# A fused three-layer block on Trainium2: the GQA value projection of the sequence tokens placed behind the key blocks, attention without a barrier, reciprocals computed on turned rows

## The chip, the cores and the metric

One core of one Trainium2 chip (trn2). The kernel is written in raw Bass: each engine has its own instruction stream, and semaphores alone order the streams. The metric is the device time in microseconds of one execution, as a median of several runs. PE is TensorE, DVE is VectorE, ACT is ScalarE, POOL is GpSimd; SP (SyncE) issues nearly all DMAs.

## The reference

One sequence of 256 tokens with 1024 features passes through a hybrid layer (Mamba-2 scan, sparse attention, a mixture of 32 experts) and then through two layers that work on the sequence (x) and on 256 context tokens: GQA with a convolutional FFN, then MLA with the same kind of FFN. All is float32. What the change touches:

```python
def rms_norm(x, g):
    return x * lax.rsqrt(jnp.mean(x * x, axis=-1, keepdims=True) + EPS) * g

def gqa_mixer(hx, hc, w_in, q_g, k_g, w_out, ctx_out):      # 16 query heads, 4 key heads, 64 wide
    def project(h):
        q, k, v = jnp.split(h @ w_in, splits, axis=-1)
        return rms_norm(q, q_g), rms_norm(k, k_g), v        # per head
    qx, kx, vx = project(hx)
    qc, kc, vc = project(hc)
    qx, kx = apply_rope(qx, cos, sin), apply_rope(kx, cos, sin)
    k_all, v_all = concat([kc, kx]), concat([vc, vx])
    out_x = softmax(qx @ k_all.T * scale) @ v_all @ w_out
    out_c = softmax(qc @ kc.T * scale) @ vc @ w_out
```

The scan's output is normed in four groups of 512 features; MLA norms its two low-rank projections.

## The kernel before

**Layout.** Activations lie feature-major: features on the 128 partitions, tokens along the columns. `hn` is the normed input, KD = 8 blocks of 128 features by 512 columns (T2), columns 0 to 255 (T) the sequence and 256 to 511 the context. Weights stream from HBM through six ring slots. SP waits for a slot to be freed (by PE or DVE) and issues the next DMA. `bank[0..7]` are the eight PSUM banks.

**A norm.** ACT squares (L1396), PE multiplies the squares with a matrix of ones (`sums`, L673), so that every partition holds the same sum for a token, ACT takes the square root into `rstd` (L1399), DVE takes its reciprocal (`norm`, L1891) and scales (L1896), ACT adds the shift (L1416) and PE uses `hn` block by block. Of these norms four are over 256 columns (first layer, before the experts, before the second FFN, the final one) and two over 512 (before the first FFN, before MLA). The scan does the same per group (`normed`, L2092, four times 256), MLA for its two projections (L2493 with 512, L2506 with 256), and between the experts and GQA two norms are done at once (L2433 and L2439, 256 each).

**GQA.** SP issues the value weights and the four `gqa` weight blocks between 921.2 and 923.4 us. PE computes the values for token tiles t = 2, 3 (context) and 0, 1 (sequence), eight matmuls each over the features, into banks 7 and 6; ACT copies both to `gva` (L1674) and signals `v_ready`. The context half of `hn` is ready early, the sequence half comes from the double norm. Then come twelve blocks c = 0 to 11: for each of KVG = 4 groups two blocks of query heads and one of keys. `block_step` is a software pipeline that stands on PE, ACT and DVE alike. At step c PE does the projection of block c into bank c % 3 (L647), for block c-1 the sum of squares within heads, **sums(c-1)** (L1191, bank 3), and for block c-2 the rope's rotation, **rot(c-2)** (L1197, bank 4). ACT squares block c (L1681) and takes the square root, **std(c-1)** (L1686, L1688). DVE takes the reciprocal, **recip(c-1)** (L2463), scales (L2466, then `q_normed`), and ropes block c-2 (L2472, L2474, L2476, then `q_roped`); L2474 needs rot(c-2). rot(c-2) waits for `q_normed` of the block after it and, since bank 4 is used again, for the rope of the block before. Steps 12 and 13 have no projection and only drain the pipeline. Then `end_phase()` makes PE, ACT and DVE wait for one another.

**Attention.** 32 pairs of heads and query tiles, again a pipeline: PE computes scores (L1213), DVE their maximum (L1976), ACT the exponentials (L1457), DVE the reciprocal of their sum and the scaling (L1984, L1992), PE transposes (L752), ACT copies (L1443), PE multiplies with the values (L1220). Scores(p) from the third pair on wait for the exponentials of pair p-2. The first pair's scores open the pipeline.

What sets the order is the program text of each engine; nothing is scheduled by a planner. The change touches the setup of the arena places (L397), PE's values, `block_step`, the barrier and `gqa_pair` (L1164 to L1222), ACT's copy (L1674) and barrier, and on DVE `norm`, `normed`, the double norm, `block_step`, the barrier and MLA's two reciprocals.

## Time and profile before

| what | us |
|---|---|
| median of 3 runs (2117.36 to 2120.48) | 2120.43 |
| the profiled execution | 2118.72 |
| its span, first to last instruction | 2116.9 |
| PE busy | 1971.0 (93%) |
| PE weight loads busy (beside PE) | 1382.5 (65%) |
| DVE busy | 1046.8 (49%) |
| ACT busy | 561.2 (27%) |
| chain that ended last: PE, DVE, DMA, waiting for nothing shown, ACT | 87%, 5%, 3%, 2%, 1% |
| mean granted clock of TensorE, share of full | 0.971 |

The profile records one execution. Busy time counts what an engine executes; the chain of work follows the last instruction back through whatever released it. The list of waits tells for each engine what it stood idle for and which instruction ended that. A name with q (DVEq) is the engine's own queue: a drain or a semaphore step of that engine ended the wait. Matmuls on float32 are recorded twice each, so 8 matmuls are 16 records. The granted clock is the share of TensorE's full 2.4 GHz; its low level, 1.2 GHz, is 0.5.

### The profile page before, as it was taken

The page shows a single profiled execution, that of the slowest core. Times are in us where ns is not written, and L with a number is a line of the kernel's source. Part 1 is how long each engine was busy: PE and PEld are TensorE (multiplying, and loading weights), DVE is VectorE, ACT ScalarE, POOL GpSimd, SP SyncE. Part 2 cuts the span into 40 slices and gives each one's busy share as a digit, 9 for nine tenths or more (in the row PEclk, how much of TensorE's full clock was granted, in tenths as well). Part 3 has the DMA queues.
Part 4 walks back from the last instruction along what each step waited for, and adds up shares of the span by engine and source line. Part 5 has one row for each costly group of instructions (what it writes and reads, how often), then busy time and mean ns, then how long its engine had stood idle before and what let it go on. Part 6 is the DMA issues. An engine that isn't in the chain of part 4 may idle for free.

```text
span 2116.9 us, 27563 instructions
## 1 busy us (share of the span) xinstructions
PE 1971.0 (93%) x9995; PEld 1382.5 (65%) x9995; DVE 1046.8 (49%) x2212; ACT 561.2 (27%) x1177; POOL 59.5 (3%) x68
## 2 busy tenths in 40 slices
PE   5999898789989999999799899999999898999997
PEld 4888687657755555564355388888444465778886
DVE  3466662367432222245676867777688334333311
ACT  3333300153131111131174133333000224443410
POOL 0000000000000000000000000101000010000000
PEclk9999999889999999999899999999999999999999
DMA  9345383232559999830102312223575020134451
GB/s 385 136 193 223 127 359 127 76 144 96 203 215 413 424 425 422 359 152 0 40 1 105 134 60 90 88 79 134 213 298 198 11 82 22 41 126 151 164 195 38
DMA packets 39465, 357.26 MB, mean 169 GB/s; under 512 B 4295, under 2 KB 9038, under 8 KB 10318
## 3 DMA queue, kind: packets, MB, share of 16 engines
q1 hardware_dynamic: 39374, 356.04, 43.1%
q8 instruction: 58, 0.95, 0.2%
q14 instruction: 33, 0.27, 0.0%
HBM read 354.97 MB, written 1.05 MB: 168 GB/s over the span
## 4 chain that ended last, share of the span: by engine, by line
PE 87%; DVE 5%; DMA 3%; issue 2%; ACT 1%; DVEq 1%; PEldq 1%; PEld 1%; SPq 0%; ACTq 0%
PE bank L647 45%; PE bank L1328 13%; PE bank L1115 6%; PE bank L1100 4%; PE bank L1137 3%; PE bank L752 2%; DMA ring<-in_ada 2%; PE bank L1300 1%; PE bank L1213 1%; PE bank L673 1%; PE bank L1220 1%; PE bank L1076 1%; PE bank L1307 1%; DMA ring<-in_q 1%; PE bank L850 1%
## 5 line engine op out<-in xcount | busy, mean ns | idle before, releaser
L647 PE MATMUL bank<-hn,ring 128*128 128x256 f32 (+2 forms) x2080 | 518.5, 409 | 13.6 <-ACT hn L1416 9.7
L647 PE MATMUL bank<-arena,ring 128*128 128x256 f32 (+2 forms) x1600 | 469.8, 451 | 24.0 <-issue 13.0
L647 PEld LDWEIGHTS bank<-hn,ring 128*128 128x128 f32 (+1 forms) x2080 | 397.2, 192 | 123.8 <-issue 69.4
L647 PEld LDWEIGHTS bank<-arena,ring 128*128 128x128 f32 (+1 forms) x1600 | 299.4, 189 | 187.7 <-issue 154.8
L1328 PE MATMUL bank<-hn,ring 128*128 128x256 f32 x704 | 161.0, 382 | 6.2 <-ACT hn L1416 6.2
L1328 PEld LDWEIGHTS bank<-hn,ring 128*128 128x128 f32 x704 | 134.6, 191 | 25.6 <-issue 7.0
L1871 DVE SCALAR_TENSOR_TENSOR bank<-ring,c_rows 128x1024 f32<-128x1024 f32 x96 | 118.1, 1230 | 34.0 <-DMA ring<-in_ada 28.7
L1328 PE MATMUL bank<-ring 128*128 128x256 f32 x528 | 124.2, 386 | 3.2 <-DVEq L2626 3.2
L1871 DVE SCALAR_TENSOR_TENSOR ring<-ring,c_rows 128x1024 f32<-128x1024 f32 x96 | 117.1, 1220 | 0.0
L1328 PEld LDWEIGHTS bank<-ring 128*128 128x128 f32 x528 | 101.8, 194 | 18.9 <-issue 3.9
L2396 DVE COPY ring<-bank 128x128 f32<-128x128 f32 x39 | 11.4, 293 | 204.3 <-PE bank L1122 204.3
L1396 ACT ACTIVATE hn<-resid 128x256 f32<-128x256 f32 (+1 forms) x48 | 22.6, 485 | 338.6 <-DVE resid L1950 338.6
L1950 DVE SCALAR_TENSOR_TENSOR resid<-bank,ada,resid 128x256 f32 x56 | 25.6, 481 | 147.3 <-PE bank L647 144.9
L2567 DVE TENSOR_TENSOR ring<-ring,bank 128x256 f32<-128x256 f32 x154 | 59.7, 418 | 60.7 <-PE bank L1328 56.0
L2613 DVE SCALAR_TENSOR_TENSOR ring<-bank,cols,ring 128x255 f32<-128x255 f32 x88 | 40.4, 480 | 90.1 <-ACT ring L1768 86.4
L1100 PE MATMUL bank<-ring,arena 64*128 64x256 f32 x624 | 77.9, 388 | 1.8 <-ACT arena L1653 1.8
L1745 ACT ACTIVATE ring<-ring,cols 128x512 f32<-128x512 f32 x44 | 35.8, 813 | 159.4 <-DVE ring L2567 159.4
L1137 PE MATMUL bank<-ring 128*64 128x512 f32 x312 | 75.5, 605 | 0.0
L752 PEld LDWEIGHTS bank<-consts,ring 128*128 128x128 f32 x416 | 47.7, 146 | 41.3 <-DVE ring L1992 32.4
L1115 PE MATMUL bank<-ring,arena 128*64 128x256 f32 x640 | 72.6, 379 | 0.5 <-DVE ring L2396 0.5
L1443 ACT ACTIVATE ring<-bank 128x512 f32<-128x512 f32 (+1 forms) x128 | 59.7, 520 | 45.8 <-PE bank L752 45.6
L2562 DVE SCALAR_TENSOR_TENSOR ring<-ring,cols 128x510 f32<-128x510 f32 x88 | 63.1, 747 | 14.6 <-issue 10.4
(408 smaller groups left out, 2154.1 us busy)
## 6 DMA issues: line engine op xcount, KB each, us to landing
ring<-in_ada SPq DMA_DIRECT2D x28, 2048.0 KB, 8.5
ring<-in_up SPq DMA_DIRECT2D x44, 1024.0 KB, 4.9
ring<-in_egu SPq DMA_DIRECT2D x20, 2048.0 KB, 10.8
ring<-in_edn SPq DMA_DIRECT2D x39, 1024.0 KB, 9.4
ring<-in_down SPq DMA_DIRECT2D x16, 1408.0 KB, 10.1
arena<-in_egu SPq DMA_DIRECT2D x10, 2048.0 KB, 10.7
hn<-in_egu SPq DMA_DIRECT2D x9, 2048.0 KB, 10.9
ring<-in_adat SPq DMA_DIRECT2D x8, 2048.0 KB, 12.5
```

The source lines that it names most:

```text
L647: last = mm(out, lhs(i), rhs(i), start=i == 0, stop=i == k - 1)
L752: last = tr(bank[4 + e][:, x * P:(x + 1) * P], probs[t % 3][:, e, c:c + P], ident)
L1100: last = mm(moe_sum(4 * half + m), y_sb[v % 2][rows, m * P:(m + 1) * P], s_t[v % 2][rows, :], start=v == 0 and m % 2 == 0, stop=v == ITEMS ...
L1115: last = mm(bank[x][64 * q:64 * q + 64, 0:T], x_t[x][:, k, :] if i else xs[:, k, 0:CAP], w_gate_up(i % 4)[:, k * 512 + q * T:k * 512 + (q ...
L1137: last = mm(bank[6 + x][64 * half:64 * half + 64, :], he_t[:, x, k * CAP:(k + 1) * CAP], w_down(v % 4)[:, k * D + half * 512:k * D + half ...
L1328: last = mm(bank[4 * q + b][:, 0:T], lhs[:, k, :], rhs(k), start=k == 0, stop=k == 3)
L1443: fn(probs_t[t % 2][:, e, 0:w], banks[:, 4 + e, 0:w], ACT.Copy).then_inc(s["att_PT"], 1)
L1745: fn(ffn_acc[:, 2 * q + x, :], up_u[q][:, x, :], ACT.Identity, scale=cols[:, ds(j + (cw + 2 * FB + x * FB), 1)], bias=cols[:, ds(j + (cb + ...
L1871: V.scalar_tensor_tensor(products, w, 1.0, c_row if layer == 0 else c_rows[:, v, :], ALU.mult, ALU.mult, accum_out=sums[x][:, b, v:v + 1])
L2562: V.scalar_tensor_tensor(aa, uu, cols[:, ds(j + (cw + tap * 2 * FB + x * FB), 1)], aa, ALU.mult, ALU.add)
L2567: V.tensor_tensor(out, one, other, ALU.add).then_inc(s["up_added"], 1)
L2613: V.scalar_tensor_tensor(aa, uu, cols[:, ds(j + (cw + tap * 2 * FB + x * FB), 1)], aa, ALU.mult, ALU.add)
```

## The change

Four things are different.

1. PE computes only the context tokens' values (t = 2, 3) ahead of the blocks. `values_of(0)` stands behind block 11's step, `values_of(1)` behind step 12. Block 0 takes `hn` with a wait per feature block. ACT copies bank 7 (context) where it copied both, and bank 6 behind its last `block_step`.
2. `end_phase()` behind the blocks becomes `end_phase(False)` on PE, ACT and DVE: each signals, none waits. In its place each value product waits for `v_ready` 2, and the scores of the last KV group wait for the sixteenth `q_roped`.
3. A function `inverse(rows, w, turned, few)` on DVE transposes the rows in 32x32 squares into `turned`, takes the reciprocal of one column in 32 into `few` (w/32 columns), and transposes `few`, repeated 32 times, back.
4. `inverse` is called where a reciprocal over 256 or 512 columns stood, except at L2416 (context half, during the experts). Space: `turned` and `few` in the arena and in `spare`, or parts of `hn` and other tiles that are free at that moment.

```diff
@@ PE
-                    for t in (2, 3, 0, 1):
-                        if t % 2 == 0:
-                            n["hn_ready"] += KD
-                        last = dot(bank[6 + t // 2][:, (t % 2) * T:(t % 2 + 1) * T], lambda k: hn_block(k)[:, t * P:(t + 1) * P],
+                    def values_of(t):
+                        return dot(bank[6 + t // 2][:, (t % 2) * T:(t % 2 + 1) * T], lambda k: hn_block(k)[:, t * P:(t + 1) * P],
                                    lambda k: slot(0)[:, k * T:(k + 1) * T], KD)
-                    last.then_inc(s["v_mm"], 1)
-                    free(0)
-                    taken(1, 0)
+                    n["hn_ready"] += KD
+                    values_of(2)
+                    values_of(3).then_inc(s["v_mm"], 1)
+                    n["hn_ready"] += KD
...
-                                lambda k: hn[:, k, :], KD).then_inc(s["q_mm"], 1)
+                                lambda k: hn[:, k, :] if since(c, 1) else hn_block(k), KD).then_inc(s["q_mm"], 1)
...
-                    for b in range(2):
-                        block_step(b, KVG)
-                    end_phase()
+                    values_of(0)
+                    block_step(0, KVG)
+                    values_of(1).then_inc(s["v_mm"], 1)
+                    free(0)
+                    taken(1, 0)
+                    block_step(1, KVG)
+                    end_phase(False)
...
+                            if g == KVG - 1:
+                                pe.wait_ge(s["q_roped"], 3 * KVG + 4)
...
                         def values(out, pt):
+                            pe.wait_ge(s["v_ready"], 2)
@@ ACT
-                    for x in range(2):
-                        last = fn(gva[:, 2 * x:2 * x + 2, :], bank[6 + x][:, :], ACT.Copy)
-                    last.then_inc(s["v_ready"], 1)
+                    fn(gva[:, 2:4, :], bank[7][:, :], ACT.Copy).then_inc(s["v_ready"], 1)
...
                     block_step(0, KVG)
-                    end_phase()
+                    act_e.wait_ge(s["v_mm"], 2)
+                    fn(gva[:, 0:2, :], bank[6][:, :], ACT.Copy).then_inc(s["v_ready"], 1)
+                    end_phase(False)
@@ DVE
+            def inverse(rows, w, turned, few):
+
+                n_few = w // 32
+                V.transpose(turned[:, 0:w], rows)
+                ve.drain()
+                V.reciprocal(few[:, 0:n_few], turned[:, 0:w].rearrange("p (b c) -> p b c", c=32)[:, :, 0])
+                ve.drain()
+                V.transpose(rows.rearrange("p (b c) -> p b c", c=32), few[:, 0:n_few].unsqueeze(2).to_broadcast([P, n_few, 32]))
+                ve.drain()
...
-                V.reciprocal(rstd[:, 0:w], rstd[:, 0:w])
-                ve.drain()
+                inverse(rstd[:, 0:w], w, hn[:, KD - 1, :], hn[:, KD - 2, 0:16])
...
-                            V.reciprocal(gq_std[:, x, :], gq_std[:, x, :])
-                            ve.drain()
+                            inverse(gq_std[:, x, :], T2, turned, few)
...
-                    end_phase()
+                    end_phase(False)
```

PE at the end of GQA's blocks, before. L1191 is sums, L1197 rot, L1213 the scores, L752 the transposes, L647 a projection.

```order
L647 MATMUL bank<-hn,ring 128x512 x7
L1191 MATMUL bank<-arena,consts 128x512 [waits q_std,q_sq]
L1197 MATMUL bank<-arena,consts 128x256 [waits q_roped,q_normed]
L1191 MATMUL bank<-arena,consts 128x512 [waits q_std,q_sq]
L1197 MATMUL bank<-arena,consts 128x256 [waits q_roped,q_normed] x2
L1213 MATMUL bank<-arena 128x512 [waits phase_ended]
L1213 MATMUL bank<-arena 128x512
L1213 MATMUL bank<-arena 128x256 x2
L1213 MATMUL bank<-arena 128x512 [waits att_exp]
L1213 MATMUL bank<-arena 128x512
L752 MATMUL bank<-consts,ring 128x128 [waits att_scaled]
```

The same place after the change (sums are L1192, rot L1198, scores L1220, transposes L753, projections and values L648).

```order
L648 MATMUL bank<-hn,ring 128x512 x7
L1192 MATMUL bank<-arena,consts 128x512 [waits q_std,q_sq]
L1198 MATMUL bank<-arena,consts 128x256 [waits q_roped,q_normed]
L648 MATMUL bank<-ring,hn 128x256 [waits hn_ready] x8
L1192 MATMUL bank<-arena,consts 128x512 [waits q_std,q_sq]
L1198 MATMUL bank<-arena,consts 128x256 [waits q_roped,q_normed]
L648 MATMUL bank<-ring,hn 128x256 [waits hn_ready] x8
L1198 MATMUL bank<-arena,consts 128x256 [waits q_roped,q_normed]
L1220 MATMUL bank<-arena 128x512 x2
L1220 MATMUL bank<-arena 128x256 x2
L1220 MATMUL bank<-arena 128x512 [waits att_exp]
L1220 MATMUL bank<-arena 128x512
```

Eight value matmuls stand ahead of sums(11) and eight behind rot(10), and the first scores have no wait of their own.

ACT where attention begins, before and, in the second block, after. L1457 (after: L1465) is attention's exponential, with the load of its table ahead of it; L1704 is the second copy of the values.

```order
L1686 ACTIVATE arena<-bank,consts 128x512 [waits q_ss]
L1688 ACTIVATE arena<-bank,consts 128x512 [waits q_ss]
L1457 ACT_TABLE_LOAD [waits att_max]
L1457 ACTIVATE ring<-bank,ring 128x512 [waits phase_ended]
L1457 ACTIVATE ring<-bank,ring 128x512
L1457 ACTIVATE ring<-bank,ring 128x256 [waits att_max]
```

```order
L1692 ACTIVATE arena<-bank,consts 128x512 [waits q_ss]
L1694 ACTIVATE arena<-bank,consts 128x512 [waits q_ss]
L1704 ACTIVATE arena<-bank 128x512 [waits v_mm]
L1465 ACT_TABLE_LOAD
L1465 ACTIVATE ring<-bank,ring 128x512 [waits att_max]
L1465 ACTIVATE ring<-bank,ring 128x512
```

The table load has lost its wait for `att_max`, which now stands on the first exponential, and the copy is in front of it.

DVE around the last two GQA blocks, after the change; before, one RECIPROCAL of 128x512 stood in place of each three rows L1900, L1902, L1904.

```order
L1900 STREAM_TRANSPOSE arena<-arena 128x512 [waits q_std]
L1902 RECIPROCAL ring<-arena 128x16
L1904 STREAM_TRANSPOSE arena<-ring 128x512
L2480 SCALAR_TENSOR_TENSOR arena<-bank,cols,arena 128x512
L2486 TENSOR_TENSOR arena<-arena,consts 128x256
L2488 TENSOR_TENSOR arena<-bank,consts 128x256 [waits q_rot]
L2490 TENSOR_TENSOR arena<-arena 128x256
L2486 TENSOR_TENSOR arena<-arena,consts 128x256
L2488 TENSOR_TENSOR arena<-bank,consts 128x256 [waits q_rot]
L2490 TENSOR_TENSOR arena<-arena 128x256
L1993 TENSOR_REDUCE ring<-bank 128x2 [waits att_S] x2
L2001 RECIPROCAL ring<-ring 128x2 [waits att_exp]
```

The rope of the block before keeps its place behind the scaling (L2480), and attention's maxima (L1993) no longer wait for the phase.

## Rows read from the trace of the kernel before

**Rows 1.** Waits of PE: engine, line, releaser, us in total, times, longest us.
```profile
PE bank L647 <- ACT hn L1416: 13.3, 3, 6.2
PE bank L1197 <- DVEq L2477: 9.0, 2, 4.5
PE bank L647 <- DVEq L1838: 8.2, 4, 4.6
...
PE bank L1328 <- ACT hn L1416: 6.2, 1, 6.2
...
PE bank L859 <- DVE ring L2124: 3.5, 1, 3.5
```

**Rows 2.** Groups on DVE: line, operation, names, shapes, count, busy us, mean ns, idle before.
```profile
L2463 DVE RECIPROCAL arena<-arena 128x512 f32<-128x512 f32 x12 | 40.2, 3353 | 47.0 <-ACT arena L1686 39.1 <-ACT arena L1688 7.8
...
L2092 DVE RECIPROCAL ring<-ring 128x256 f32<-128x256 f32 x4 | 7.0, 1753 | 7.6 <-ACT ring L1502 7.3
L1891 DVE RECIPROCAL rstd<-rstd 128x256 f32<-128x256 f32 x4 | 7.0, 1752 | 11.7 <-ACT rstd L1399 11.6
...
L1891 DVE RECIPROCAL rstd<-rstd 128x512 f32<-128x512 f32 x2 | 6.7, 3352 | 10.9 <-ACT rstd L1399 10.9
```

**Rows 3.** The same view, other operations on DVE.
```profile
L2472 DVE TENSOR_TENSOR arena<-arena,consts 128x256 f32<-128x256 f32 x12 | 5.1, 427 | 1.4
...
L2110 DVE TENSOR_TENSOR ring<-arena 128x512 f32<-128x512 f32 x4 | 2.8, 691 | 0.3
...
L2102 DVE COPY ring<-arena 128x512 f32<-128x512 f32 x4 | 1.7, 427 | 0.3
...
L2238 DVE RECIPROCAL arena<-arena 128x8 f32<-128x8 f32 x4 | 0.8, 203 | 0.3
```

**Rows 4.** Timeline of PE, at 593 us and at 1702 us: start, us, instructions.
```profile
593.29 3.64 PE L647 MATMUL bank<-hn,w_route 128*36 128x256 f32 x16
...
1701.87 4.84 PE L647 MATMUL bank<-arena,ring 128*96 128x256 f32 x16
```

**Rows 5.** Chain of work where GQA begins: start, us, what.
```profile
932.36 14.05 PE bank L647 x64
```

**Rows 6.** Timeline of ACT beside it: start, us, instructions, idle before and releaser.
```profile
936.02 3.30 ACT L1407 ACTIVATE hn<-hn,ada 128x256 f32<-128x256 f32 x8 [2.89 <-DVE hn L2444]
```

**Rows 7.** The line that issues the four gqa DMAs, us to landing.
```profile
DMA to landing us min/median/max: 8.2/13.0/17.5
```

**Rows 8.** Chain of work from GQA's last block into attention: start, us, what.
```profile
1041.65 0.87 PE bank L1191 x2
...
1042.54 0.70 ACT arena L1686
...
1043.26 3.35 DVE arena L2463
...
1046.69 0.75 DVE arena L2466
...
1048.94 3.35 DVE arena L2463
...
1054.67 1.21 PE bank L1197 x2
...
1057.00 2.10 PE bank L1213 x4
...
1060.50 1.28 ACT L1457
1061.79 1.46 ACT ring L1457 x4
...
1063.29 1.59 PE bank L1213 x4
...
1067.66 0.59 PE bank L752 x4
```

**Rows 9.** Two stretches: length, busy us by engine, granted clock, DMA share, GB/s.
```profile
1057.00:1062.00 5.00, 2.93 (x8) 1.19 (x8) 1.82 (x2) 1.49 (x2) 0.00 (x0) 0.66 0.01 2
1062.00:1067.00 5.00, 3.71 (x14) 2.16 (x16) 2.96 (x7) 2.94 (x10) 0.00 (x0) 0.68 0.00 0
```

More of the change, by code:

```diff
@@ L399, in build @@
         inv_final, rstd_final = gq_cos, gq_sin
+        turned, few = pl(T2), spare[:, 0:16]
         gain_squared, gain_both = mod[2][:, 0, 0, :], mod[2][:, 0, 1, :]
@@ L2091, in normed @@
                 ve.wait_ge(s["ssm_std"], g + 1)
-                V.reciprocal(rs_ssm, rs_ssm)
-                ve.drain()
+                inverse(rs_ssm, T, ysq, ysq[:, T:T + 8])
                 for b in range(4):
@@ L2432, in _ @@
             ve.drain()
-            V.reciprocal(inv_final, inv_final)
+            inverse(inv_final, T, turned, few)
             ve.drain().then_inc(s["two_inv"], 1)
@@ L2438, in _ @@
             ve.wait_ge(s["two_std"], 1)
-            V.reciprocal(rstd[:, 0:T], rstd[:, 0:T])
-            ve.drain()
+            inverse(rstd[:, 0:T], T, turned, few)
             V.tensor_tensor(rstd[:, 0:T], rstd[:, 0:T], rstd_final, ALU.mult)
@@ L2462, in block_step @@
                             ve.wait_ge(s["q_std"], c)
-                            V.reciprocal(gq_std[:, x, :], gq_std[:, x, :])
-                            ve.drain()
+                            inverse(gq_std[:, x, :], T2, turned, few)
                             gain = VO["gqa_q_norm_g_2"] if x < 2 else VO["gqa_k_norm_g_2"]
@@ L2492, in _ @@
                     ve.wait_ge(s["kv_roped"], 2)
-                    V.reciprocal(ckv_rstd[:, :], ckv_rstd[:, :])
-                    ve.drain()
+                    inverse(ckv_rstd[:, :], T2, ckv_sq[:, 0, :], ckv_sq[:, 1, 0:16])
                     for b in range(2):
@@ L2505, in _ @@
                     ve.wait_ge(s["kv_roped"], 3)
-                    V.reciprocal(rstd[:, 0:T], rstd[:, 0:T])
-                    ve.drain()
+                    inverse(rstd[:, 0:T], T, ckv_sq[:, 0, :], ckv_sq[:, 1, 0:16])
                     for b in range(3):
```

## The prediction, made before the changed kernel was run

> **What bounds the kernel now.** TensorE (PE) is busy for 93% of the span, so I read first who makes it wait. The list of PE's waits [rows 1] holds few long ones, and each has VectorE (DVE) or ScalarE (ACT) in front of it at a place where a statistic is inverted: 13.3 us in three waits for the shifted norm, 6.2 us in one more of the same kind before the FFN, 3.5 us in the scan, up to 4.6 us at the scan's end, and 9.0 us in two waits for the last rope steps of GQA. Next come the reciprocals [rows 2]: 3.35 us for 512 columns, 1.75 us for 256. The difference over 256 columns is 1.60 us, so 6.25 ns a column and about 0.15 us fixed. A reciprocal of 8 columns takes 0.20 us [rows 3]; 16 columns are then about 0.25 us. Last I follow the chain of work from GQA's last block into attention [rows 8]: from the end of the sums at 1042.52 to the transposes of the second pair at 1067.66 PE has 6.6 us of work of its own.
>
> **Part one: the turned reciprocal.** All rows of such a statistic that are inverted are equal within each 32 partitions, so a 32x32 turn leaves w/32 different numbers a partition. `inverse` is transpose, reciprocal of w/32 columns, transpose back, with drains between. No DVE transpose is in the trace. Nearest are the operations that pass one element a cycle: 0.427 us for 256 columns and 0.691 us for 512, the latter with a broadcast operand as the second transpose has [rows 3]; they give 1.03 ns a column and 0.16 us fixed. The lower bound is the copy of 512 columns at 0.427 us (256 would be about 0.29); the upper one is twice the time per column, 0.69 and 1.22 us. I take the one-element rate, since a transpose moves each element once and is four-byte data. Between dependent DVE operations lie about 0.07 us (1043.26 + 3.35 = 1046.61, next start 1046.69 [rows 8]).
> - 256 columns: 2 x 0.427 + 0.20 + 2 x 0.07 = 1.19 us against 1.75: saves 0.56. Bounds 0.82 and 0.03.
> - 512 columns: 2 x 0.691 + 0.25 + 0.14 = 1.77 us against 3.35: saves 1.58. Bounds 2.10 and 0.52.
>
> The Trainium skill ("VectorE: DVE Perf Modes", The three transpose paths) gives 311 ns for a 128x128 bf16 transpose; my estimate from that page is 0.44 us for 256 columns and 0.71 for 512, by which part one would be 5.7 us in place of the 6.0 below. The same page's rules for kernel authors say to minimise the count of chained DVE operations because each is drained; here one operation becomes three, and the trace prices that rule at the 0.16 us fixed and 0.07 us between that are in the sum.
>
> Which of the calls end a wait? 256 columns: the first norm, the scan's third and fourth group (PE waits 3.5 and 4.6 us right behind them [rows 1]), the norm before the second FFN, and the final norm, which is followed only by the scaling and the output's DMA. 5 x 0.56 = 2.8 us. The scan's first two groups count nothing, since no PE wait of any size names them. 512 columns: the norm before the first FFN and the one before MLA, 2 x 1.58 = 3.2 us. Nothing is gained where PE is busy anyway: the norm before the MoE (PE starts the router at 593.29 right behind the context's sums, without idle [rows 4]), the two in the double norm before GQA (PE starts at 932.36 right behind its own sums), MLA's two (PE starts the heads at 1701.87 without idle [rows 4]). If that cover were gone, each would again be worth its 0.56. Behind each shortened norm the next to be late is the same DVE to ACT chain (scale, shift), which moves along. **Part one: 6.0 us**, bounds 8.3 and 1.2.
>
> **Part two: the order in GQA.** Four value projections of 8 matmuls take 14.05 us [rows 5], 3.51 each. Two of them (sequence tokens) leave the front, so block 0 starts 7.02 us sooner, at 939.38. It now needs the sequence half of `hn`: ACT shifts it from 936.02 to 939.32, one eighth each 0.41 us [rows 6], and block 0's matmuls of 512 columns take 0.88 us per eighth, twice those of the values, so there is no wait. It needs the first `gqa` weights: four DMAs issued from 921.7, landing after 8.2 to 17.5 us [rows 7], the first thus by 930 and the last by 941, where group 3 is wanted after 1000. ACT's copy of the values is split, with cover on both sides. No queue is passed by a DMA: slot 0 is freed later, and the streams that follow go to slots 1 and 3 and, after the phase, to 5 and 4.
>
> At the tail, sums(c), rot(c), std(c) and recip(c) are block c's steps; times of before less 7.02 [rows 8]: sums(10) end at 1035.50 and rot(9) at 1035.93. Then:
> - values(0), 3.51: to 1039.44; sums(11), 0.87: to 1040.31.
> - On DVE, recip(10) could start at 1036.24. Before, from one reciprocal's start to the rot that it releases were 1054.67 - 1048.94 = 5.73 us, of which 2.38 is not reciprocal. So rot(10) is released at 1036.24 + 1.77 + 2.38 = 1040.39: no wait to speak of. values(1) ends at 1044.3.
> - std(11) is done at 1040.31 + 0.74 = 1041.05; rot(11) is released at 1041.05 + 1.77 + 2.38 = 1045.20. PE waits 0.9 us, in place of 4.5 twice.
> - Scores follow at once (1045.63), since only the last KV group's pairs wait for the last rope; before, they waited for all engines until 1057.00.
> - The first scores took 2.10 us at the half clock (granted 0.66 over the stretch [rows 8, 9]); PE has been busy, so I take 1.05: to 1046.68. From there to ACT's table load, with DVE's maximum between, were 1.40 us: to 1048.08. In ACT's order the table load, 1.28 us on the chain before, now waits for no maximum: it runs behind the copy, at 1044.9 to 1046.2. Exponentials 1.46 and 0.04 to PE: scores(2) start at 1049.6, not 1063.29. From them to transposes(1) were 4.37 us at a granted clock of 0.68 [rows 8, 9]; at the full one I take 2.7, between half of it and 0.68 of it: 1052.3. Before: 1067.66.
>
> **Part two: 15.3 us** (2.7 of it from the shorter reciprocals). What is late next is the chain max, exp, scale of the first pair, with PE idle 2.3 us. From there the attention runs at PE's pace as before. Added on PE are one wait per value product and one on each of the last eight score groups; they ride on matmuls that wait for `att_PT` or `att_exp` anyway, and rows with two such waits show no gap: nothing. Is more than 15.3 possible? With the copy's rate 15.8. At the half clock behind the 2.3 us of idle, the step from scores(2) to transposes(1) stays at 4.37 us, 1.6 more: 13.7.
>
> Sum: 2118.72 (span 2116.9 and 1.8 around it) - 6.0 - 15.3 = 2097.4. The median of the runs is 1.7 us above the profiled one; I meet it halfway: **2098**.
>
> **The rivals.**
> 1. The transpose passes an element in two cycles. For: it reorders through a store, and all data are four bytes. Against: every other row without division goes at one a cycle or faster. Part one is then 1.2 us. At the tail rot(10) is released at 1041.4 and rot(11) at 1046.6: 13.9 us. In all 15.1: 2104.
> 2. The gain is made and partly lost again: half clock at the start of attention (1.6), and the three gains before 260 us (1.7) end at a DMA-fed stretch. For: the clock was 0.66 to 0.68 in this place [rows 9]. Against: PE's idle time here falls to a fraction, and SyncE waits for slots that PE and DVE free, so transfers move with them. 2101.
> 3. The order doesn't do what it says: block 0 waits for weights that land together, not in turn, by 940.9. 1.6 us: 2100. Against: the first landed after 8.2 us [rows 7].
> 4. Slower: the DVE transpose is as slow as its reciprocal, an element in several cycles. With x us for 512 columns, part one gives 13.0 - 10.2x, the tail 18.8 - 4x; the sum is zero at x = 2.2 us. At the reciprocal's own 3.35 us the kernel is at least 16 us slower, 2135 or more, and DVE with 7.1 + 2.4 us a block would outlast PE's 7.0 of projection, 0.9 of sums and 0.4 of rot. For: 6.25 ns a column exists on this engine. Against: that is division; nothing is divided here.
>
> **How the numbers follow.** Forecast 0.67, with its own range 2095 to 2100. Rival 1 0.14, rival 2 0.10, rival 3 0.04, rival 4 0.05, of which 0.02 near its zero point. The range runs from the copy's rate (2118.7 - 8.3 - 15.8 = 2094.6), less 2 us for places where a shorter wait may spare PE a half clock (it costs 1.6 us at one such place above), to rival 1 with a little: 2092.5 to 2105. About 0.2% (4 us) is what a measurement of this kernel tells from no change. Faster 0.95, same 0.02, slower 0.03.
>
> **What would show it.** In the profile after: two DVE transposes of about 0.43 us (256) and 0.69 (512) per inverse; PE's waits for the shifted norm 0.5 or 1.6 us shorter each; block 0 of GQA 7.0 us behind the start of the values and without a wait; no PE wait over 1 us between the last block and the first scores; ACT's table load before the first maximum; the first scores at about 1.05 us. Wrong it would be by a transpose over 1 us, by a wait on `hn` or a `gqa` landing ahead of block 0, or by a half clock through the first pairs.

## The result, and the profile after

The changed kernel takes 2105.1 us (2103.83 to 2108.05, 4 runs) against 2120.45; the ratio is 0.9933, 95% interval [0.992, 0.9946]. It is faster by 15.3 us, where 21 to 22 were forecast, and lies 0.1 us outside the range of 2092.5 to 2105. (Run again it took 2103.16 us, so on which side of 2105 it falls is chance; that it misses the forecast by 5 to 7 us is not.) The profiled execution took 2108.05 us, the slowest of the four. The page of it, span, busy time by engine and chain by engine:

```profile
span 2106.2 us, 27701 instructions
...
PE 1979.1 (94%) x9995; PEld 1389.3 (66%) x9995; DVE 1016.2 (48%) x2264; ACT 561.2 (27%) x1177; POOL 59.4 (3%) x68
...
PE 90%; DVE 3%; issue 2%; ACT 1%; DMA 1%; PEld 1%; PEldq 1%; DVEq 0%; SPq 0%; ACTq 0%
```

The kernel before had PE busy for 1971.0 us in a span of 2116.9, with the same 9995 matmuls. So PE's time without work fell from 145.9 to 127.1 us, by 18.8, and the same matmuls took 8.1 us longer. The span is 10.7 us shorter where the sum had 21.3: 2.5 of the difference are time without work that did not go, and 8.1 are matmuls that took longer. The rest of this text looks for where the 8.1 us are and why.

The waits of PE (engine, line, releaser, us in total, times, longest), to be read against [rows 1]:

```profile
PE bank L648 <- ACT hn L1424: 10.8, 3, 4.6
PE bank L648 <- DVEq L1846: 7.7, 4, 4.1
...
PE bank L1336 <- ACT hn L1424: 4.6, 1, 4.6
...
PE bank L860 <- DVE ring L2140: 3.0, 1, 3.0
PE bank L1220 <- ACT ring L1465: 2.4, 1, 2.4
```

Each wait is shorter by what the sum had: three waits for the shifted norm by 2.5 us (0.56 + 1.58 + 0.56 = 2.7 forecast), the one before the FFN by 1.6, the scan's by 0.5 each. Of the 9.0 us of rope waits 1.2 are left. The pieces that `inverse` is made of, on DVE (line, operation, shapes, count, busy us, mean ns, idle before), stand against [rows 2]:

```profile
L1904 DVE STREAM_TRANSPOSE arena<-ring 128x512 f32<-128x512 f32 x12 | 8.5, 712 | 1.3 <-issue 0.4
...
L1902 DVE RECIPROCAL ring<-arena 128x16 f32<-128x16 f32 x12 | 3.0, 254 | 1.2 <-issue 0.4
...
L1904 DVE STREAM_TRANSPOSE rstd<-hn 128x256 f32<-128x256 f32 x4 | 1.8, 446 | 0.3
...
L1902 DVE RECIPROCAL hn<-hn 128x8 f32<-128x8 f32 x4 | 0.8, 204 | 0.3
```

A transpose is 0.712 us for 512 columns and 0.446 for 256, where 0.691 and 0.427 were taken. GQA's tail on PE's timeline (start, us, instructions, idle before and releaser), to be read against [rows 8]:

```profile
1044.61 0.67 PE L1198 MATMUL bank<-arena,consts 128*128 128x256 f32 x2 [0.22 <-DVEq L2491]
1045.12 3.62 PE L648 MATMUL bank<-ring,hn 128*128 128x256 f32 x16
1049.70 0.67 PE L1198 MATMUL bank<-arena,consts 128*128 128x256 f32 x2 [0.97 <-DVEq L2491]
1050.48 1.56 PE L1220 MATMUL bank<-arena 64*128 64x512 f32 x8
1054.41 1.43 PE L1220 MATMUL bank<-arena 64*128 64x512 f32 x4 [2.37 <-ACT ring L1465]
1055.77 1.97 PE L753 MATMUL bank<-consts,ring 128*128 128x128 f32 x8
```

The two waits for rope are 0.2 and 0.97 us, value products fill the space between, and the first scores start 0.78 us after the last rotation starts, with no barrier. ACT's table load stands ahead of the first maximum, at 1049.46, as forecast:

```profile
1048.77 0.60 ACT L1704 ACTIVATE arena<-bank 128x512 f32<-128x512 f32 x1 [3.66 <-PE bank L648]
1049.46 1.28 ACT L1465 ACT_TABLE_LOAD   x1
1052.91 0.69 ACT L1465 ACTIVATE ring<-bank,ring 128x512 f32<-128x512 f32 x1 [2.16 <-DVE ring L1993]
```

What the sum did not have (rival 2 did) is the last row on PE: eight transposes take 1.97 us, and the granted clock there is 0.66 (columns: length, busy us of PE, its loads, DVE, ACT, POOL, clock, DMA share, GB/s), nearly what [rows 9] had:

```profile
1055.00:1060.00 5.00, 5.00 (x33) 3.21 (x30) 3.31 (x9) 3.09 (x10) 0.00 (x0) 0.66 0.00 0
```

**Where the time went, stretch by stretch.** The sums of each norm (L673 before, L674 after) and the router are marks that both timelines have. Rows of before, then of after:

```profile
18.51 5.79 PE L673 MATMUL bank<-hn,consts 128*128 128x256 f32 x16 [3.23 <-ACT hn L1396]
...
1201.40 7.12 PE L673 MATMUL bank<-hn,consts 128*128 128x512 f32 x16 [0.38 <-issue]
...
1646.63 7.13 PE L673 MATMUL bank<-hn,consts 128*128 128x512 f32 x16 [0.41 <-issue]
...
1860.42 3.71 PE L673 MATMUL bank<-hn,consts 128*128 128x256 f32 x16 [0.38 <-issue]
...
2102.24 3.71 PE L673 MATMUL bank<-hn,consts 128*128 128x256 f32 x16 [0.38 <-issue]
```

```profile
18.08 6.75 PE L674 MATMUL bank<-hn,consts 128*128 128x256 f32 x16 [3.24 <-ACT hn L1404]
...
597.53 3.64 PE L648 MATMUL bank<-hn,w_route 128*36 128x256 f32 x16
...
1192.41 7.12 PE L674 MATMUL bank<-hn,consts 128*128 128x512 f32 x16 [0.38 <-issue]
...
1635.33 7.12 PE L674 MATMUL bank<-hn,consts 128*128 128x512 f32 x16 [0.38 <-issue]
...
1847.95 3.71 PE L674 MATMUL bank<-hn,consts 128*128 128x256 f32 x16 [0.38 <-issue]
...
2092.12 3.71 PE L674 MATMUL bank<-hn,consts 128*128 128x256 f32 x16 [0.38 <-issue]
```

The router of before starts at 593.29 [rows 4]. Six stretches follow, the first from the end of the first sums: 568.99, 608.11, 445.23, 213.79, 241.82 and 14.66 us in the kernel before. The table has what the same marks give in every kernel run here, less those of before; the experiments are told below. The last column is the span less PE's busy time; in the four kernels with dummy matmuls (`warm_` and `fit_`) the dummies count as busy.

| kernel | to router (scan, first attention) | to norm before FFN 1 (MoE, GQA) | to norm before MLA | to norm before FFN 2 | to final norm | tail | PE without work |
|---|---|---|---|---|---|---|---|
| forecast | -1.7 | -15.3 | -1.6 | -1.6 | -0.6 | -0.6 | |
| after | +3.7 | -13.2 | -2.3 | -1.2 | +2.4 | -0.6 | 127.1 |
| after_again | +2.3 | -13.3 | -2.3 | -1.1 | +2.4 | -0.5 | 128.7 |
| before_again | -0.2 | -0.2 | +0.1 | 0.0 | 0.0 | -0.1 | 145.8 |
| turn_only | +4.6 | -3.4 | -2.7 | -1.4 | -0.6 | -0.6 | 136.0 |
| order_only | -0.3 | -11.2 | -1.2 | -3.5 | +1.7 | -0.1 | 136.9 |
| early_turn | +3.1 | -0.3 | +0.1 | +0.1 | -0.1 | -0.1 | 145.4 |
| early_longer | +2.7 | +0.1 | 0.0 | 0.0 | 0.0 | +0.3 | 148.7 |
| late_turn | +0.8 | -13.4 | -2.8 | -1.2 | +2.4 | -0.6 | 129.4 |
| warm_before | -3.0 | -0.8 | -1.3 | -1.8 | +1.4 | -0.1 | 123.5 |
| warm_after | +0.5 | -13.6 | -2.8 | -1.7 | +1.4 | -0.6 | 112.0 |
| fit_turned | -2.2 | -15.0 | -1.9 | -3.8 | -0.5 | +0.4 | 114.4 |
| fit_plain | +0.9 | -15.1 | -1.4 | -3.9 | 0.0 | +0.9 | 120.0 |

Two stretches carry the miss: the first lost 3.7 us where 1.7 were to be won, and the fifth lost 2.4. In the fifth the clock of the matmuls behind the norm shows it, first in the kernel before and then after:

```profile
1870.00:1875.00 5.00, 5.00 (x25) 4.41 (x24) 0.48 (x1) 2.18 (x3) 0.00 (x0) 1.00 0.00 0
```

```profile
1855.00:1860.00 5.00, 5.00 (x13) 3.92 (x13) 1.78 (x5) 2.35 (x6) 0.00 (x0) 0.50 0.00 0
```

PE waits 3.55 us for `hn` before and 3.04 after, and then does 25 matmuls in 5 us at 2.4 GHz before, 13 at 1.2 GHz after. A wait 0.5 us shorter was followed by half clock, where the longer one was not.

### The profile page after: what moved, and what is told of

It reads as the page before. It is cut to its first block, busy times and chain, and to the rows that moved or that the text cites. A ratio compares the mean times of both kernels' runs of the same rounds, so it can differ in the third digit from the quotient of the medians.

```text
span 2106.2 us, 27701 instructions
## 1 busy us (share of the span) xinstructions
PE 1979.1 (94%) x9995; PEld 1389.3 (66%) x9995; DVE 1016.2 (48%) x2264; ACT 561.2 (27%) x1177; POOL 59.4 (3%) x68
## 4 chain that ended last, share of the span: by engine, by line
PE 90%; DVE 3%; issue 2%; ACT 1%; DMA 1%; PEld 1%; PEldq 1%; DVEq 0%; SPq 0%; ACTq 0%
PE bank L648 48%; PE bank L1336 13%; PE bank L1116 6%; PE bank L1101 4%; PE bank L1138 3%; PE bank L753 2%; PE bank L674 2%; PE bank L1308 1%; PE bank L1220 1%; PE bank L1228 1%; PE bank L1077 1%; PE bank L851 1%; PE bank L1315 1%; DMA ring<-in_q 1%; PE bank L1019 1%
## 5 line engine op out<-in xcount | busy, mean ns | idle before, releaser
L648 PE MATMUL bank<-hn,ring 128*128 128x256 f32 (+2 forms) x2080 | 525.3, 413 | 11.0 <-ACT hn L1424 7.7
L648 PE MATMUL bank<-arena,ring 128*128 128x256 f32 (+2 forms) x1600 | 470.2, 451 | 23.4 <-issue 13.7
L648 PEld LDWEIGHTS bank<-hn,ring 128*128 128x128 f32 (+1 forms) x2080 | 402.1, 194 | 122.9 <-issue 66.9
L648 PEld LDWEIGHTS bank<-arena,ring 128*128 128x128 f32 (+1 forms) x1600 | 299.7, 189 | 187.2 <-issue 155.5
L1336 PEld LDWEIGHTS bank<-ring 128*128 128x128 f32 x528 | 101.2, 193 | 18.8 <-issue 3.9
L2412 DVE COPY ring<-bank 128x128 f32<-128x128 f32 x39 | 11.4, 293 | 204.1 <-PE bank L1123 204.1
L753 PEld LDWEIGHTS bank<-consts,ring 128*128 128x128 f32 x416 | 48.0, 146 | 40.8 <-DVE ring L2009 32.1
L2574 DVE SCALAR_TENSOR_TENSOR ring<-ring,cols 128x510 f32<-128x510 f32 x88 | 63.2, 748 | 14.4 <-issue 10.2
```

Of the source, the lines that this page charges most:

```text
L648: last = mm(out, lhs(i), rhs(i), start=i == 0, stop=i == k - 1)
L753: last = tr(bank[4 + e][:, x * P:(x + 1) * P], probs[t % 3][:, e, c:c + P], ident)
L1336: last = mm(bank[4 * q + b][:, 0:T], lhs[:, k, :], rhs(k), start=k == 0, stop=k == 3)
L2574: V.scalar_tensor_tensor(aa, uu, cols[:, ds(j + (cw + tap * 2 * FB + x * FB), 1)], aa, ALU.mult, ALU.add)
```

## The experiments

Two theories. P, the prediction's: what a wait loses, the kernel wins. B: TensorE's stretches at 1.2 GHz lie at fixed places for one stream of instructions, and each edit moves them, so the span changes by the waits plus what these stretches gain or lose. The theory A of the first expectations is that they fall at random from one execution to the next.

**Repeats.** `after_again` is the changed kernel and `before_again` the kernel before, both unedited.

> The changed kernel itself, once more, with its own profile. Theory A (the granted clock falls to its half level in different places from execution to execution, and this ate some 6 us of the gain): the time is again 2103 to 2108, and the stretches at half clock do not stand all in the same places as in the first profile; in particular the start of the second FFN (0.68 and 0.64 granted there, where the kernel before had 1.00) may be back at 1.00, which is worth 2.4 us. Theory B (the loss belongs to the changed instruction streams): the same places at half clock, and shift by shift the same times as in the first profile within 0.5 us.

> The kernel before, once more, for a second profile. Theory A expects its half-clock stretches to move too: some of the stretches 41 to 60, 226 to 245, 385 to 460 and 1864 to 1875 us show another granted clock than 0.75, 0.91, 0.67 to 1.00 and 1.00. Theory B expects the same granted clock within 0.03 in each.

Measured: after_again 2103.16 us, ratio 0.992 [0.9906, 0.9934]; before_again 2118.36, ratio 0.9999 [0.999, 1.0009]. In the table before_again stands within 0.2 us of before in all six stretches, and after_again within 0.1 us of after in the last five. Between two single profiles the stretches of half clock thus repeat; A falls for these eleven. One part does differ, the first stretch of the changed kernel, by 1.4 us.

Other executions show that A keeps a part of the truth. Each has its time and its mean granted clock on record, and within one kernel the two go together: `turn_only` took 2109.09 to 2110.23 us in its four executions at 0.975, and 2118.16 and 2118.39 in the two at 0.969; the changed kernel run again took 2098.97 and 2099.3 at 0.976 and 2105.17 to 2105.74 at 0.972 to 0.973. So the time at half clock does change from one execution to the next with the same instructions, by up to 9 us of span, and a single profile shows one draw.

**One part alone.** `turn_only` is the kernel before with every `V.reciprocal` of the diff as `inverse`. `order_only` is the changed kernel with

```
             def inverse(rows, w, turned, few):
-                n_few = w // 32
-                V.transpose(turned[:, 0:w], rows)
...
+                V.reciprocal(rows, rows)
                 ve.drain()
```

> The kernel before with the turned reciprocals alone; order and barrier of GQA as before. By the durations of the first profile after (0.71 and 0.45 us a transpose) the shortened waits sum to 5.7 us outside GQA (5 x 0.52 and 2 x 1.54) and, with the barrier in place, two serial reciprocals in GQA's tail to 3.1: 8.8 us, 0.9958. Theory A expects less by whatever half clock appears: 3 to 9 us faster, 0.996 to 0.9985. Theory B (gain lost in the instruction streams around the transposes): under 3 us.

> The changed kernel with a plain reciprocal where the turned one stood: order of GQA and missing barrier alone. From the tail of the kernel before: two value products move into the gap; rot(10) is released at about 1042.0 and rot(11) at 1047.8 in the forecast's times, so 12.6 us less; with a half clock at attention's start 1.6 less than that. Expected 10.5 to 13 us faster, 0.994 to 0.995, and PE waits of 1.6 and 2.3 us for the two last rotations. If this and the turned reciprocals alone add up to clearly more than both together (15.3 us), the two parts overlap in the tail by about 3 us as the steps of the forecast say.

Measured: turn_only 2113.62 us, ratio 0.9973 [0.9963, 0.9983], 5.0 us won. order_only 2104.27, ratio 0.993 [0.9917, 0.9943], 14.4 won, 1.4 more than its highest expectation. On top of the order the turned reciprocals bring about 1 us (15.5 of after_again less 14.4), which the intervals of the two ratios don't tell from nothing; the prediction had 6.0 + 2.7 = 8.7 us for them. PE's line on the page of turn_only, then of order_only:

```profile
PE 1976.9 (94%) x9995; PEld 1385.6 (66%) x9995; DVE 1015.8 (48%) x2264; ACT 561.4 (27%) x1177; POOL 59.4 (3%) x68
```

```profile
PE 1964.6 (93%) x9995; PEld 1379.5 (66%) x9995; DVE 1046.9 (50%) x2212; ACT 561.5 (27%) x1177; POOL 59.5 (3%) x68
```

With spans of 2112.9 and 2101.5, PE without work is 136.0 and 136.9 us: 9.9 and 9.0 less than before. Together 18.9, and the kernel with both has 18.8 less in its first profile and 17.1 less in its second (128.7 against 145.8). So time without work adds up to 1 or 2 us. Busy time does not: +5.9 and -6.4 alone, +8.1 together (+4.6 in the second profiles). order_only won 3.5 us between the norms before MLA and before FFN 2, where it has the same instructions as the kernel before; that is a stretch of clock that came along, and no merit of the order.

**Only the early reciprocals, and only the late ones.** `early_turn` is the kernel before with `inverse` in the first norm (`norms[0] == 0`) and in the scan's `normed`; `late_turn` is the changed kernel with these made plain:

```
+            def plain(rows):
+                V.reciprocal(rows, rows)
+                ve.drain()
...
+                if norms[0] == 0:
+                    plain(rstd[:, 0:w])
+                else:
+                    inverse(rstd[:, 0:w], w, hn[:, KD - 1, :], hn[:, KD - 2, 0:16])
...
-                inverse(rs_ssm, T, ysq, ysq[:, T:T + 8])
+                plain(rs_ssm)
```

> The kernel before, with the turned reciprocal only in the first norm and in the scan's two group norms (all before 460 us), nothing else changed. By the prediction's sum (theory P) this alone gives 3 x 0.56 = 1.7 us: about 2118.7. Theory B (the stretches in which TensorE is granted 1.2 GHz have fixed places for one instruction stream, and are moved and added to by the shorter waits): the records of the changed kernel and of turned reciprocals alone stand 4.7 and 5.4 us later after 460 us than those of the kernel before, once the gaps there are summed, so this kernel is slower than the one before by 1 to 5 us, about 2123, with most of the loss between 370 and 460 us in stretches at a granted clock under 0.9. After 500 us its segments equal those of the kernel before within 0.5 us by either.

> The changed kernel with the plain reciprocal put back in the first norm and in the scan's two group norms; the turned one stays in the GQA blocks, the norms before the feed-forwards, MLA and the end. Theory P: three waits grow by 0.56 us, so it is 1.7 us slower than the changed kernel. Theory B: its first 460 us are those of the kernel before (the GQA order alone had them within 0.6 us), its later segments those of the changed kernel, so the last records come 3 to 5 us earlier than in the changed kernel: 2100 to 2103, ratio to the changed kernel's about 0.998.

Measured: early_turn 2120.77 us, ratio 1.0006 [0.9997, 1.0016]: no gain from three waits each half a microsecond shorter. P's 1.7 us would be a ratio of 0.9992, below the interval. Its profile shows 3.1 us more in the first stretch, and at most 0.3 anywhere else; its times spread from 2115.09 (granted 0.973) to 2125.74 (0.968). late_turn 2104.05, ratio 0.9929 [0.9916, 0.9942]. Its first stretch is 2.9 us shorter than that of after (1.5 shorter than that of after_again) and its other five are those of after within 0.5, as B wanted, but against the changed kernel's 0.992 of its own comparison that is no gain by the times. P's 1.7 us loss isn't seen either.

Where early_turn loses can be read from one group of 32 matmuls, first in the kernel before and then in early_turn:

```profile
381.70 7.14 PE L647 MATMUL bank<-hn,ring 128*128 128x256 f32 x32 [0.70 <-DVEq L1838]
```

```profile
381.07 8.69 PE L647 MATMUL bank<-hn,ring 128*128 128x256 f32 x32 [0.70 <-DVEq L1838]
```

It starts 0.63 us sooner, so up to here the shorter waits are still won, and it lasts 1.55 us longer behind the same wait. The windows from 380 to 390 us (shape as above) of before, after, early_turn and late_turn:

```profile
380.00:390.00 10.00, 8.55 (x45) 7.07 (x46) 2.61 (x27) 1.04 (x2) 0.00 (x0) 1.00 0.00 0
```

```profile
380.00:390.00 10.00, 8.52 (x42) 7.05 (x40) 2.18 (x26) 0.56 (x2) 0.00 (x0) 0.83 0.00 0
```

```profile
380.00:390.00 10.00, 9.06 (x39) 7.26 (x36) 2.18 (x26) 0.14 (x1) 0.00 (x0) 0.83 0.00 0
```

```profile
380.00:390.00 10.00, 8.65 (x45) 7.10 (x45) 2.18 (x26) 0.41 (x3) 0.00 (x0) 1.00 0.00 0
```

No instruction of those 10 us is edited. In these four the granted clock is 0.83 where the early reciprocals are turned and 1.00 where they are plain; the repeats have 0.85 (after_again) and 1.00 (before_again). The place is not the same in every kernel with turned ones: turn_only has 1.00 there and lost its 4.6 us mostly further on, where the kernel before (first row) has a better clock than it (second):

```profile
447.00:457.00 10.00, 8.45 (x60) 4.96 (x60) 8.12 (x47) 8.77 (x36) 0.00 (x0) 0.83 0.01 2
```

```profile
447.00:457.00 10.00, 7.78 (x38) 4.65 (x40) 7.27 (x45) 7.90 (x32) 0.00 (x0) 0.65 0.01 2
```

So up to the first attention turn_only and the changed kernel hold the same instructions on every engine, and still differ in where they lose: the first stretch is the one that repeats least.

**The same waits made longer.** `early_longer` is the kernel before with, ahead of each of the scan's reciprocals and, with other tiles, of the first norm's,

```
+                V.reciprocal(ysq[:, 0:64], rs_ssm[:, 0:64])
+                ve.drain()
                 V.reciprocal(rs_ssm, rs_ssm)
```

> The kernel before with one more reciprocal of 64 columns (about 0.55 us by 6.25 ns a column and 0.15 fixed, 0.6 with the gap) in the first norm and in each of the scan's group norms, so each of the waits that early_turn shortened by 0.56 us is longer by 0.6 us instead. Theory P (a wait's length is what counts): 3 x 0.6 = 1.8 us slower than before, and the segments without a changed wait keep their lengths. Theory B (a shift of the instruction stream moves and resizes the half-clock stretches): segments between 370 and 600 us that hold no changed wait change by 0.5 to 2 us either way, so the total is off 1.8 by a few us; if only shorter waits do harm, there is no such change.

Measured: 2123.16 us, ratio 1.0018 [1.0009, 1.0027], so 3.8 us slower, 1.9 to 5.7. PE without work is 2.8 us more (1.8 expected), and the profile's first stretch 2.7 longer. By the timelines of the two kernels 2.0 of it have come by 60 us: 0.6 are a longer wait for a weight DMA (1.37 us against 0.77), 0.6 the wait that was made longer (4.25 against 3.62), and the rest half clock behind it (granted 0.69 from 38 to 60 us, against 0.77). The other waits add 1.2. From 262 to 440 us, where early_turn lost over 3 us, every matmul starts 2.2 to 2.5 us after the same one of the kernel before, and from 370 to 600 us the unedited part ends up 0.5 shorter. That is the low end of the 0.5 to 2 us that B allowed, although the whole stream came over 2 us later. So a shift by itself doesn't cost: here P is about right, and the sign of B's part cannot be foretold from the length of a wait.

**Filling the waits.** `warm_after` and `warm_before` are the two kernels with dummy matmuls, 12 behind the last `ada_cols` of the first norm, 16 behind `norm(T2)`, 16 and 12 behind `norm(w)` of the two FFNs, 8 in GQA's attention:

```
+            def keep_on(count):
+                for _ in range(count):
+                    mm(bank[5][:, 0:2 * P], ones, consts[:, 0:2 * P], start=True, stop=True)
...
                         pairs[p].scores(bank[x], bank[x + 1]).then_inc(s["att_S"], 1)
+                        if p == 1 and N == 32:
+                            keep_on(8)
```

> The changed kernel with dummy matmuls (128x256, ones times constants, into a bank that nobody reads) in TensorE's waits: 12 behind the last column product of the first norm, 16 behind the sums of the norms before MLA and before the first feed-forward, 12 before the second, 8 behind the second scores of the attention's start. At full clock 12 of them are 2.6 us, less than the waits they stand in. Theory B: what the changed kernel lost there is half clock behind those waits (about 0.7 us at 40 us, 1.2 at 1055, 2.3 at 1855), so 3 to 6 us go, and the time is 2099 to 2102. If the losses were not the clock, the time is that of the changed kernel or up to 3 us more, since a dummy that is still running delays the first true matmul.

> The kernel before with the same dummy matmuls at the same five places. Its records show full clock behind the norm at 1867 us and half clock around 40 us and in the attention's start; theory B: it gains less than the changed kernel does from them, 0 to 4 us (2116 to 2120), so that the difference of the two filled kernels is 16 to 19 us. If the fillers gave both the same, the difference stays at 15.3.

Measured: warm_after 2101.9 us, ratio 0.9907 [0.9894, 0.992]; warm_before 2113.29, ratio 0.9972 [0.996, 0.9983]. Both won, but the kernel before won more (5.5 us) than the changed one (1.6: 16.9 us under the kernel before, where 15.3 stood without fillers), against the expectation, so the pair is 11.4 us apart and not 16 to 19. One reason is in the fillers: a 128x256 dummy is recorded twice, 0.22 us apart, so 12 of them last 5.3 us and cover the turned norm (PE waited 3.04) and the plain one (3.55) alike; what the turned one saves is lost to the dummies. PE's time without work says the same: 123.5 and 112.0 us, 11.5 apart in place of 18.8, while its busy time is 1987.8 and 1988.1. That the busy times agree is a sum of unlike parts, though: warm_before is granted 0.50 from 1044 to 1057 us, at the end of GQA's blocks. warm_after has its half clock in the first attention, where no filler stands, and there its first stretch loses the 3.5 us by which it is the longer of the two. The windows from 447 to 457 us of warm_before, then of warm_after:

```profile
447.00:457.00 10.00, 9.94 (x78) 6.00 (x76) 8.17 (x45) 8.23 (x33) 0.00 (x0) 0.87 0.01 2
```

```profile
447.00:457.00 10.00, 10.00 (x52) 6.16 (x52) 4.76 (x28) 5.76 (x22) 0.00 (x0) 0.50 0.01 2
```

`fit_turned` has fillers cut to the waits: 6, 9, 9 and 6 in the four norms, 4 in GQA's and 4 in the first attention, with the plain reciprocal in the scan. `fit_plain` is the same with the plain reciprocal in `norm`:

```
-                inverse(rstd[:, 0:w], w, hn[:, KD - 1, :], hn[:, KD - 2, 0:16])
+                V.reciprocal(rstd[:, 0:w], rstd[:, 0:w])
+                ve.drain()
```

> The changed kernel with the plain reciprocal put back in the scan's two group norms, and with dummy matmuls cut to the waits (one of them runs as two passes of 0.22 us, as the filled kernels showed, 12 = 5.4 us): 6 in the first norm, 9 before MLA and before the first feed-forward, 6 before the second, 4 in the start of GQA's attention and 4 in the start of the first attention (at 443 us). Theory B: from 2104.0 (plain reciprocals up to 460 us) the half clock behind these waits goes: about 3.0 in the first norm, 2.7 before MLA (64 matmuls took 27.4 us there, 24.7 when filled), 2.3 before the second feed-forward, 1 in GQA's attention: 2093 to 2097. If the fillers only delay, 2104 or more.

> The same with the plain reciprocal also in the six norms (first, routing, before MLA, before both feed-forwards, final). The prediction's sum (theory P) takes each of the three norms over 256 columns or less at 0.56 us and the two over 512 at 1.58: with the routing one 4 x 0.56 + 2 x 1.58 = 5.4 us slower than its partner. Theory B: with the clock held by the dummies the shorter waits count in full except before the first feed-forward, where a second wait of 3.3 us follows that ends with VectorE: 3.8 to 5.4 us slower than its partner, though without dummies the same reciprocals brought at most 1 us on top of the order.

Measured: fit_turned 2095.83 us (2092.55 to 2097.86), ratio 0.9894 [0.988, 0.9908], faster than both kernels of this case: 22.1 us less than the one before. fit_plain 2100.88, ratio 0.9922 [0.9909, 0.9935]: the turned norms are worth 5.1 us here, where 3.8 to 5.4 were expected. How the clock is kept is seen in the norm before MLA, PE's timeline of late_turn (no filler) and then of fit_turned:

```profile
1631.33 7.12 PE L674 MATMUL bank<-hn,consts 128*128 128x512 f32 x16 [0.38 <-issue]
1643.09 27.43 PE L648 MATMUL bank<-hn,ring 128*128 128x512 f32 x64 [4.64 <-ACT hn L1424]
```

```profile
1634.43 4.05 PE L680 MATMUL bank<-consts 128*128 128x256 f32 x18
1639.24 24.78 PE L648 MATMUL bank<-hn,ring 128*128 128x512 f32 x64 [0.76 <-ACT hn L1433]
```

The dummies fill 4.05 of the wait, and the same 64 matmuls take 24.8 us and not 27.4. Their granted clock, in the first 10 us of late_turn and then of fit_turned:

```profile
1643.00:1653.00 10.00, 9.91 (x17) 4.33 (x18) 4.95 (x14) 5.65 (x15) 0.00 (x0) 0.73 0.00 0
```

```profile
1639.00:1649.00 10.00, 9.76 (x23) 4.46 (x24) 5.09 (x14) 6.30 (x16) 0.00 (x0) 1.00 0.00 0
```

The pair also corrects the expectation. Time without work falls by 5.6 us from fit_plain to fit_turned, against P's 5.4, but by stretch the profile puts 3.1 of the difference ahead of the router, where the first norm's 0.6 was due (1.1 with the routing one), 0.5 each in the third (1.6 due), the fifth and the last, and none in the fourth, where 1.6 was due. So part of the agreement of 5.1 with the sum is luck. Even with most of the clock held, waits do not turn into span one for one.

The Trainium skill ("TensorE: Matmul & The Clock Gate", Part 1) holds, of the slow matmuls with which a kernel starts, that the same kernel meets a different number of them from run to run, and that they cost under 1% of a span and shouldn't be fitted. The slow matmuls here stand in the middle of a kernel. In part they behave alike: early_turn and turn_only spread over 9 to 11 us with their granted clock, and the first stretch of the changed kernel differs by 1.4 us between profiles. In part they don't: in two kernels profiled twice, eleven of twelve stretches kept their length within 0.2 us. And dummies won 7.4 us (late_turn is 14.8 us under the kernel before in its own comparison, fit_turned 22.1), of which at most 0.6 is the first norm's reciprocal: under 1% indeed, but half of what this change brings.

## Why the prediction was wrong, step by step

- **Price of `inverse`: right.** 1.82 us measured for 512 columns (2 x 0.712 + 0.254 + 0.14) against 1.77, and 1.24 against 1.19 for 256. Rival 1 (two cycles an element) and rival 4 (as slow as division) fall.
- **Which waits shrink: right.** 9.9 us of PE's time without work go in turn_only; the sum's 6.0 and two GQA waits of 1.6 (the old order keeps both) make 9.2. Nothing was gained where PE had cover.
- **GQA's order: right in kind, high by 2.0.** 13.2 to 13.3 us were measured for 15.3. Block 0 started 6.98 us behind the values and without a wait, so rival 3 falls. Waits for rope were 0.2 and 0.97 us, forecast 0 and 0.9. The scores start 0.78 us after the last rotation starts, where 0.43 was taken, and one reciprocal on DVE was held 0.4 us. Most of the rest is rival 2's half clock behind the third scores: with four dummies there the eight transposes take 1.09 us and not 1.97, and the stretch is 15.0 us shorter, so it cost about 1.7, against 1.6 put on that rival. (The 6.6 us of own work that the prediction read for PE between 1042.52 and 1067.66 are too few, as PE is busy for 11.19 us there; no term of the sum rests on them.)
- **Waits turned into time: the step that failed.** "5 x 0.56 = 2.8 us" and "2 x 1.58 = 3.2 us" were taken from the span in full, with the clock elsewhere left as it was. The first stretch got 3.7 us longer in place of 1.7 shorter, and the one behind the second FFN's norm 2.4 longer in place of 0.6 shorter. Both are matmuls at 1.2 GHz that had run at 2.4 GHz. The first goes with the early reciprocals: the four profiles that have them turned and no fillers (after, after_again, turn_only, early_turn) are 2.3 to 4.6 us longer there, the three that have them plain and unlengthened (before_again, order_only, late_turn) -0.3 to 0.8. The loss behind the second FFN's norm comes with the new order: 2.4 us in after, after_again and late_turn, and 1.7 in order_only, whose norm is not shortened, but none in turn_only, whose norm is. Rival 2, at 0.10, came nearest: it named this loss of the early gains, but laid it to a DMA-fed stretch, where the runs show half clock, and its price was the gain itself (1.7), where the loss against the forecast was 4.0 to 6.3.
- **The sum against the medians.** The two profiles differ by 10.7 us (12.5 for the repeats) and the medians by 15.3 to 15.5. The profiled execution of the changed kernel was the slowest of its four runs (2108.05, granted 0.970; the others had 0.973), so some of what the table shows as lost is not in every run. The granted clocks of the other executions say how much half clock they had, but not where.

What stays open: by which rule a change of half a microsecond puts a half-clock stretch here and not there. The kernels with changed early waits lost 3.1 (shorter) and 2.7 us (longer, of which 1.8 are the waits themselves), so neither direction is sure to gain, and no run tells which places will be hit.

## What to carry to other kernels

Compare the busy time of the bounding engine for the same instructions, not the span alone: here idle time added up over two edits to 1 or 2 us (9.9 + 9.0 against 18.8 and 17.1) while the time of the same matmuls moved by -6 to +8 us. Read the granted clock of every execution beside its time before a single profile is believed. Price a shortened wait at its length, but widen the range by the half clock that the kernel already has around its waits, some 2 us a place, in both directions. And where PE waits 3 to 5 us for a norm, dummy matmuls that end just before the wait does were worth 7.4 us, about half of the whole change; longer ones eat what they save.

## What the runs showed of the hardware

- The DVE transpose of 32x32 blocks moves four-byte data at 1.04 ns a column (0.446 us for 256, 0.712 for 512), even when it reads through a broadcast operand, while the reciprocal needs 6.25 ns a column.
- A 3 us wait of PE was followed by 25 matmuls in 5 us in one kernel and 13 in another, with the same instructions and a wait only 0.5 us different.
- Edits of half a microsecond each between 38 and 255 us went with a granted clock of 0.83 to 0.85 instead of 1.00 at 380 to 390 us, where nothing is edited, in three of four profiles; waits made longer by 0.6 us at the same places left it at 1.00.
- With the same instructions the mean granted clock differs between executions, and the time with it: 0.975 and 2109 to 2110 us, 0.969 and 2118 us (`turn_only`).
- An fp32 dummy matmul of 256 columns is recorded twice, and the records start 0.22 us apart at full clock (24 records in 5.34 to 5.43 us).
